# Streaming the adaLN modulation behind the feed-forward blocks, with unrolled linear stages and waits per PSUM set

## What is computed

```python
def modulation(cond, ada_w, ada_b):              # cond: (1, 1024), ada_w: (1024, 9 * 1024)
    m = jax.nn.silu(cond) @ ada_w + ada_b
    return jnp.split(m[:, None, :], 9, axis=-1)

def layer(x, cond, l, latent, st):               # once for context tokens, once for latent tokens
    sh1, sc1, gt1, sh2, sc2, gt2, sh3, sc3, gt3 = modulation(cond, ada_w[l], ada_b[l])
    h = rms_norm(x, norm_g[l, 0]) * (1 + sc1) + sh1
    x = x + 0.5 * gt1 * swiglu(h, ffn_w1[l, 0], ffn_w2[l, 0])     # 1024 -> 2 * 2816 -> 1024
    h = rms_norm(x, norm_g[l, 1]) * (1 + sc2) + sh2
    # two mixers on h @ w_in (layer 0: retention, RWKV-7; layer 1: mLSTM, attention), then @ w_out
    x = x + gt2 * mix
    h = rms_norm(x, norm_g[l, 2]) * (1 + sc3) + sh3
    x = x + 0.5 * gt3 * swiglu(h, ffn_w1[l, 1], ffn_w2[l, 1])
    return x, new
```

## Time and profile before

| | us |
|---|---|
| median of 3 runs | 3899.51 |
| lowest, highest | 3883.81, 3903.02 |
| the profiled execution's own time | 3888.84 |
| its span, first to last instruction | 3887.0 |

### The profile page before, as it was taken

The page is one execution under the profiler, slowest core; times in us unless marked ns, Lnnn a source line. Parts: engine busy times, 40 slices in busy tenths (PEclk is TensorE's granted clock), DMA queues, the critical chain, the costliest instruction groups (busy, mean ns, idle before and its releaser), DMA issues.

```text
span 3887.0 us, 52585 instructions
## 1 busy us (share of the span) xinstructions
PE 3428.2 (88%) x21383; PEld 3045.3 (78%) x21383; DVE 1267.6 (33%) x1862; ACT 996.1 (26%) x1361; POOL 336.1 (9%) x366
## 2 busy tenths in 40 slices
PE   8799998969577877899999979999897689899998
PEld 1399998959466665899998169999897656899998
DVE  0222222245455554322221032222314435322222
ACT  0232122222321122332120033122224435332121
POOL 0000001000444441100000000000101000100001
PEclk9899999969788887999999989999997879999999
DMA  8522121101000000122222822122110100122121
GB/s 312 174 76 77 60 86 55 34 31 50 3 4 1 1 1 22 60 76 76 65 81 78 303 90 82 64 70 81 44 49 12 33 3 27 58 73 76 65 88 42
DMA packets 79087, 260.64 MB, mean 67 GB/s; under 512 B 20112, under 2 KB 20240, under 8 KB 78704
## 3 DMA queue, kind: packets, MB, share of 16 engines
q1 hardware_dynamic: 77568, 250.79, 19.4%
q0 software_dynamic: 1392, 8.07, 0.5%
HBM read 255.02 MB, written 3.81 MB: 67 GB/s over the span
## 4 chain that ended last, share of the span: by engine, by line
PE 82%; DVE 7%; ACT 4%; POOL 3%; issue 3%; DMA 1%; DVEq 0%; SPq 0%; ACTq 0%; POOLq 0%
PE ps L1988 30%; PE ps L1989 30%; PE ps L2009 6%; PE ps L893 1%; PE ps L1817 1%; DVE normed L2266 1%; DVE h_lo L2253 1%; PE ps L884 1%; PE ps L1797 1%; DMA ring<-w_ada 1%; PE ps L1500 1%; POOL h_mem L2357 1%; PE ps L1805 1%; PE ps L873 1%; PE ps L837 1%
## 5 line engine op out<-in xcount | busy, mean ns | idle before, releaser
L315 DVE TENSOR_TENSOR w_lo<-ring,w_hi 128x1024 fp32r<-128x1024 f32 (+1 forms) x305 | 399.0, 1309 | 1867.7 <-ACT w_hi L310 1867.7
L310 ACT ACTIVATE w_hi<-ring 128x1024 fp32r<-128x1024 f32 (+1 forms) x305 | 343.0, 1126 | 1522.0 <-PE ps L1989 1501.8
L1988 PE MATMUL ps<-h_hi,w_hi 128*128 128x320 f32 x1928 | 609.7, 316 | 126.0 <-DVE h_lo L2253 58.5
L1989 PE MATMUL ps<-h_hi,w_hi 128*128 128x320 f32 x1928 | 602.3, 312 | 0.0
L1988 PE MATMUL ps<-h_lo,w_hi 128*128 128x320 f32 x1928 | 601.9, 312 | 0.0
L1989 PE MATMUL ps<-h_lo,w_hi 128*128 128x320 f32 x1928 | 601.8, 312 | 0.0
L1988 PE MATMUL ps<-h_hi,w_lo 128*128 128x320 f32 x1928 | 601.6, 312 | 0.0
L1989 PE MATMUL ps<-h_hi,w_lo 128*128 128x320 f32 x1928 | 601.5, 312 | 0.0
L1988 PEld LDWEIGHTS ps<-h_hi,w_hi 128*128 128x128 f32 x1928 | 367.2, 190 | 145.2 <-issue 80.7
L1989 PEld LDWEIGHTS ps<-h_hi,w_hi 128*128 128x128 f32 x1928 | 368.4, 191 | 0.0
L1988 PEld LDWEIGHTS ps<-h_lo,w_hi 128*128 128x128 f32 x1928 | 367.9, 191 | 0.0
(11 more groups left out here) (348 smaller groups left out, 4527.0 us busy)
## 6 DMA issues: line engine op xcount, KB each, us to landing
ring<-w_ada SPq DMA_DIRECT2D x144, 512.0 KB, 4.5
ring<-w_up0a SPq DMA_DIRECT2D x44, 512.0 KB, 3.4
ring<-w_up0b SPq DMA_DIRECT2D x44, 512.0 KB, 3.3
ring<-w_up1a SPq DMA_DIRECT2D x44, 512.0 KB, 3.3
ring<-w_up1b SPq DMA_DIRECT2D x44, 512.0 KB, 3.3
ring<-w_down0a SPq DMA_DIRECT2D x16, 704.0 KB, 4.0
ring<-w_down0b SPq DMA_DIRECT2D x16, 704.0 KB, 4.0
ring<-w_down1a SPq DMA_DIRECT2D x16, 704.0 KB, 4.1
```

Of the source, the lines that this page charges most:

```text
L310: act.activation(w_hi[:, n % SPLITS, 0:cols], ring[:, r, 0:cols], ACT.Copy).then_inc(high_ready, 1)
L315: dve.tensor_tensor(w_lo[:, n % SPLITS, 0:cols], ring[:, r, 0:cols], w_hi[:, n % SPLITS, 0:cols].bitcast(F32), ALU.subtract).then_inc(spli ...
L1988: pe.matmul(left, weights, acts[:, k, LEFT], start=start, stop=stop)
L1989: mm = pe.matmul(right, weights, acts[:, k, RIGHT], start=start, stop=stop)
```

## The change

The modulation of a layer is no longer a stage. Its nine chunks (1024 outputs, eight tiles each) are handled one at a time. Chunks 0 and 1 of layer 0 are computed at the start, before norm0. The other seven of layer 0 are interleaved with its first feed-forward part, chunks 0 to 5 of layer 1 with layer 0's second one, and the last three with layer 1's first one: behind each linear block there, TensorE multiplies one modulation tile (128 of the 144 tiles in all), whose load stands in the queue just behind that of the block's own tile. A tile is now multiplied as four matmuls of 256 columns, whose stationary operand is `scond` widened to 32 columns and whose outputs lie in four groups of 32 PSUM partitions. ScalarE copies a chunk's sums once (128 x 256), and behind the next block TensorE makes two 128 x 128 transposes and VectorE up to three small instructions.

PSUM sets go from four to three; banks 6 and 7 belong to the modulation and to the norm's sums. All loops of the linear stages are unrolled in the program text; `pairs_read` and the `free_*` semaphores are gone, and a block waits for the reader of the block three before it. A down stage's first block waits for `gated_ready` k-step by k-step. In the last block of a stage ahead of a norm, VectorE adds the residual before it splits the next tile, and ScalarE squares block u in step u (before: u-1, with the last one after the loop). At the start only 256 columns of the constants and `x` are loaded; the other constants and `lora` follow behind norm0.

```diff
-SETS = 4
+SETS = 3
+    first_chunks = [(0, m) for m in range(2)]
+    later_chunks = {(0, "up0a"): [(0, m) for m in range(2, N_MOD)], (0, "up1a"): [(1, m) for m in range(6)],
+                    (1, "up0a"): [(1, m) for m in range(6, N_MOD)]}
...
+    loads = [(c, k) for c in first_chunks for k in range(DB)]
+    for b in range(lin):
+        loads.append(b)
+        if b in ada_behind:
+            loads.append(ada_behind[b])
...
+            for n, t in enumerate(loads):
+                r = n % RING
+                if n >= RING and isinstance(loads[n - RING], tuple):
+                    sp.wait_ge(ada_used, sum(isinstance(e, tuple) for e in loads[:n - RING + 1]))
+                elif n >= RING:
+                    sp.wait_ge(split_ready, loads[n - RING] + 1)
...
+            def modulation_tile(chunk_, k):
+                q, n = chunk_no[chunk_], place[chunk_, k]
+                r = n % RING
+                if k == 0 and q:
+                    pe.wait_ge(ada_row_ready, q)
+                pe.wait_ge(land[r], landed[n])
+                for j in range(4):
+                    mm = pe.matmul(bank(6, 0, 2 * P)[32 * j:32 * j + 32], scond[:, k, :],
+                                   ring[:, r, j * 2 * P:(j + 1) * 2 * P], start=(k == 0), stop=(k == DB - 1))
+                mm.then_inc(ada_used, 1)
+            def modulation_turned(chunk_):
+                q = chunk_no[chunk_]
+                pe.wait_ge(ada_row_ready, q + 1)
+                if q:
+                    pe.wait_ge(mod_ready, q)
+                for t in range(2):
+                    ins = pe.transpose(bank(7, t * P, t * P + P), ada_row[:, t * P:(t + 1) * P], C("ident"))
+                ins.then_inc(ada_turned, 1)
...
-                b0, n0 = blk0[layer, name], tile0[layer, name]
-                pairs_read(layer, name)
...
+                for u in range(n):
+                    b = block0[layer, name] + u
+                    left, right, _ = pair(b % SETS)
+                    s = b % SPLITS
+                    if b >= SETS:
+                        reader, count = read_by[b - SETS]
+                        pe.wait_ge(readers[reader], count)
+                    pe.wait_ge(split_ready, b + 1)
...
-                looped(pe, n, one)
...
+                    if b in chunk_behind:
+                        modulation_turned(chunk_behind[b])
+                    if b in ada_behind:
+                        modulation_tile(*ada_behind[b])
...
-                            pe.wait_ge(gated_ready, HALF_F * halves + 1)
-                            linear(layer, f"down{j // 2}{half}", DB, HALF_F, g_hi, g_lo, HALF_F * halves + 2)
+                            linear(layer, f"down{j // 2}{half}", DB, HALF_F, g_hi, g_lo,
+                                   ready=(gated_ready, HALF_F * halves))
```

## The result

Before took 3901.27 us (median of 4), the changed kernel 3619.70 us (median of 4, 3611.88 to 3620.95): the ratio is 0.9283, with a 95% interval of 0.9252 to 0.9313. Forecast were 3642 us, with 3600 to 3725 as range. The profiled execution of after took 3618.63 us, with a span of 3616.7 against 3887.0: 270.3 us went, where the sum said 251.

What follows compares the result with a forecast made beforehand. TensorE's work plus its pauses was taken as the bound. 116 + 146 + 20 + 81 = 363 us won less 112 paid gave 251 off: 3638 from the profiled execution, 3648 from the median, forecast 3642, range 3600 to 3725.

Steps and rivals of the forecast that it cites:

- Start: Before the first block: squares of norm0 begin at 35 us instead of 151.19, the 22.8 us after them stay; 116 us won.
- Layer 1 and norm seams: Between layers, only a norm seam of 11.2 us remains, 146 us won; earlier square and residual at norms win 20 us.
- Pauses: Between up and down stages: twelve TensorE pauses go, with 2 us of low clock after each; 81 us won.
- The cover: Down stage's first block: 60 matmuls, 8.7 us, run before the product's last part is needed, hiding its chain with 3 us spare.
- Tiles: 128 modulation tiles behind blocks, four column groups running at once, cost TensorE 0.80 us each: 102 us paid.
- The row of the half columns: Mixer matmuls on 64 columns in before's trace: two groups run at once, and switching there and back costs 0.37 us.
- Transposes: Behind blocks: 16 pairs, four records each at 0.16 us, 0.6 us a pair; 10 us paid.
- At nothing: In the linear stages: second load per block, new waits, small copies, three sets instead of four and unrolling cost or win nothing.
- The rule on row tiles: Modulation tiles: the skill's measured factor 3.07 for four row tiles would make the sum 17 us higher.
- two groups at once: Rival, modulation tiles: the array takes only two column groups together, 55 us more, 3697 us; chance 15%.
- one after the other: Rival, modulation tiles: column groups do not overlap, 164 us more, 3806 us; chance 9%.
- straight text must wait for its instructions: Rival, unrolled linear stages: new program text arrives late; waits in every second block cost 329 us, time 3971; chance 5%.

Runs made afterwards that it cites:

- the experiment: The changed kernel, with TensorE again waiting for all of gated_ready before each of the eight down stages: 3692.57 us.
- the second execution of after: The changed kernel run and profiled once more, unaltered: 3612.69 us.
- the chunks at the start: The changed kernel with all nine modulation chunks of layer 0 computed before the first block instead of two: 3677.48 us.
- the kernel with pairs: The changed kernel with two modulation tiles behind every second block instead of one behind each: median 3597.44 us, 0.9253 of before.

## Why the prediction was right

The steps hold, each at its place: no step of the sum failed. The result lies 22 us below the forecast. By the two profiled executions 270.3 us went instead of 251; 12.8 of the 19.3 us between are sizes of terms, and 6.5 are the mixer's clock, which is luck.

- *Start.* The squares came at 35.66 where 35 was taken. The 22.8 us behind them, taken as unchanged, are 24.7 now: the six adds of GpSimd (11.51 us) run while VectorE splits the first weights, and took 9.91 in before. That the one causes the other was not tried. 113.6 instead of 116.
- *Layer 1 and norm seams.* 147.1 for 146, and 23.2 for 20: each seam gave 4.9 to 5.5 us instead of 4.3. The second half of the norm's matmuls is shorter than was taken: from its start to its last pair pass 0.65 us (580.17 to 580.82), where 1.1 was put, with the granted clock at 1.00 instead of 0.59. TensorE had worked until 0.80 us before. The earlier square and the earlier residual were not tried one by one.
- *Pauses.* 84.6 for 81. The cover has 3.7 us to spare, predicted were 3, and putting the wait back cost 58.4. Taking 2 us for the low clock after each of twelve pauses was right: 25.1 by stages for 24, and 1.95 a pause in the experiment. The idle time and the steps at the borders make the rest, 59.0 for 57.1.
- *Tiles.* The row of the half columns was the right neighbour. From it the change of shape was put at 0.37; it is 0.33 for 32 columns. A tile is 0.765 instead of 0.80: 4.5 us in 128.
- *Transposes*, the term that was mis-sized most: 0.22 us a pair instead of 0.6, 6 us in 16. The trace shows two records for each pair (36 for 18 chunks) where four were counted, and 0.11 us for each, where the row gave 0.16.
- *At nothing.* The new loads and waits were rightly put at nothing: in the parts with tiles TensorE waits for no load and no row, only for the norm's `h_lo` in the first block. The parts are 104.7 us longer, and 128 x 0.765 + 16 x 0.22 is 101.4. Of the 3.3 us between, 2.9 go with the execution: the first part is 1.65 shorter in the second execution of after (the granted clock from 75 to 90 us is 1.00 there, 0.91 here), and the third 1.23 shorter with the chunks at the start (491.80 to 490.57), with the same tiles behind it. Unrolling, put at nothing too, won 6 us in the kernel before.
- *Not in the sum.* The RWKV mixer, 6.5 us shorter than in before. Two executions of after's own text differ by as much, so nothing of it can be credited to the change.
- *The rule on row tiles.* The factor of 3.07 for four row tiles (the Trainium skill, TensorE: Matmul & The Clock Gate, Measured speedup vs the span model) would have made a tile 0.93 with the shape change taken at 0.37. For these column groups the runs show a factor of 4 (1.71 to 0.43), once the shape change is counted by itself, and 0.43 for the second tile of a visit.

Of the rivals, two groups at once measured 3661.95 us and one after the other 3753.82, with 112 of the 128 tiles so; both were forced, and neither is what the changed kernel does. That straight text must wait for its instructions is refuted by the kernel before with unrolled loops: 6 us faster, not slower.

## What to carry to other kernels

Small matrix products that are bound by loading where they stand can be cut into tiles and set behind the blocks of a stage bound by TensorE: they then cost their own matmuls and the change of the array's shape, so group them (two to a visit took 22 us more off here). Before waiting for a whole product, look for the first k-step that needs its last part; here 60 matmuls of cover ended eight pauses, and each pause had cost its idle time and some 2 us more at the lower clock. Price a step in an unfamiliar shape by the nearest row, from start to start, and split it into change and work: the change stayed and the work was shared.

## What the runs showed of the hardware

- Going from 128 columns of weights to 32 and back costs 0.33 us, however many groups and products lie between (one group, two, four; one tile or two), and going to other weights at the same width 0.02.
- Two and four column groups run at once without loss: 1.71 us of float32 products in 0.86 and 0.43, beside the 0.33.
- A stage of many short bursts differs with the granted clock: 3020 matmul records of the RWKV mixer took 552.8 us at 0.86, 559.2 at 0.84, 565.8 at 0.83 and 575.7 at 0.81, the first two of these with the same text. Where such a stage is long, a difference of 20 us between two single executions proves nothing of an edit elsewhere (the four executions of the kernel with pairs lie 22 us apart); compare it by stages.
